# The indexer's logits as three fp32r products of rounded halves instead of one fp32 product

## The reference, cut to what matters

```python
h = x * (1 + scale) + shift
z = h @ w_in                     # qa ka va ga qb kb vb gb qi ki wi
logits = einsum('bthd,bsd->bths', qi, ki) * IDX_DIM ** -0.5    # 8 heads of 64
score  = einsum('bths,bth->bts', relu(logits), wi * 8 ** -0.5)
_, idx = top_k(where(admissible, score, -inf), topk)           # 256 keys (144 for the sample)
```

## Time and profile before

| | us |
|---|---|
| median of 3 runs (lowest, highest) | 1999.81 (1998.09, 2002.83) |
| profiled execution: its time / its span | 2001.68 / 2000.0 |
| PE busy, share of the span | 1869.9, 93% |
| VectorE, ScalarE, GpSimd busy | 979.8, 626.0, 680.4 |
| three query tiles with logits beside them | 284.2 to 392.8 |
| logits of pair 3 alone | 392.8 to 420.9 |
| loop of 32 tiles | 420.9 to about 1229 |

### The profile page before, as it was taken

How to read it: one execution, slowest core, us unless ns; L and a number is a source line. 1 busy time by engine, 2 the same in 40 slices (tenths; PEclk the granted TensorE clock), 3 DMA queues, 4 the chain that set the end, 5 groups by cost and what they waited for, 6 DMA issues and landing times.

```text
span 2000.0 us, 36519 instructions
## 1 busy us (share of the span) xinstructions
PE 1869.9 (93%) x13351; PEld 1561.7 (78%) x13351; DVE 979.8 (49%) x2519; ACT 626.0 (31%) x1359; POOL 680.4 (34%) x860
## 2 busy tenths in 40 slices
PE   5799999999999999999999998989999899999992
PEld 2467887679999999999999996656665688888772
DVE  2244513467777788873000004887777133342726
ACT  1122233421111111111111116988887322122120
POOL 1122211012222222222222224866666543444741
PEclk8899999979999999999999999999999999999996
DMA  7874433113222222222222244431220233346463
GB/s 226 261 250 135 124 98 111 32 38 94 85 89 85 85 86 90 85 85 85 85 85 85 85 120 115 106 84 46 58 52 19 88 121 121 122 124 182 117 216 90
DMA packets 209716, 213.27 MB, mean 107 GB/s; under 512 B 23152, under 2 KB 167280, under 8 KB 208768
## 3 DMA queue, kind: packets, MB, share of 16 engines
q1 hardware_dynamic: 178320, 172.38, 30.4%
q10 hardware_dynamic: 29952, 35.08, 5.0%
q0 software_dynamic: 1328, 4.26, 0.7%
HBM read 181.31 MB, written 34.55 MB: 108 GB/s over the span
## 4 chain that ended last, share of the span: by engine, by line
issue 45%; PE 25%; POOL 18%; ACT 5%; DVE 4%; DMA 3%; POOLq 1%; SPq 0%; ACTq 0%; DVEq 0%
POOL w_lo L1088 8%; POOL w_lo L1137 8%; PE psum L1684 4%; PE psum L1641 3%; PE psum L1663 3%; DMA ada_ring<-in_w_ada_dram 2%; PE psum L1511 2%; PE psum L1469 2%; PE psum L1512 2%; PE psum L1513 2%; ACT p_rows L972 2%; PE psum L1550 2%; PE psum L1552 1%; PE psum L1551 1%; ACT over_z_evacuated L994 1%
## 5 line engine op out<-in xcount | busy, mean ns | idle before, releaser
L1550 PE MATMUL psum<-h_hi,w_hi 128*128 128x364 f32 (+1 forms) x1728 | 577.5, 334 | 6.9 <-POOL w_lo L1088 6.2
L1552 PE MATMUL psum<-h_lo,w_hi 128*128 128x364 f32 (+1 forms) x1728 | 567.7, 329 | 0.0
L1551 PE MATMUL psum<-h_hi,w_lo 128*128 128x364 f32 (+1 forms) x1728 | 566.0, 328 | 0.0
L1088 POOL TENSOR_TENSOR w_lo<-w_raw,w_hi 128x512 fp32r<-128x512 f32 x144 | 185.5, 1289 | 701.5 <-ACT w_hi L831 701.4
L1550 PEld LDWEIGHTS psum<-h_hi,w_hi 128*128 128x128 f32 x1728 | 325.9, 189 | 44.7 <-issue 36.8
L1551 PEld LDWEIGHTS psum<-h_hi,w_lo 128*128 128x128 f32 x1728 | 325.8, 189 | 0.0
L1552 PEld LDWEIGHTS psum<-h_lo,w_hi 128*128 128x128 f32 x1728 | 325.6, 188 | 0.0
L1137 POOL TENSOR_TENSOR w_lo<-w_raw,w_hi 128x512 fp32r<-128x512 f32 x128 | 181.5, 1419 | 209.0 <-ACT w_hi L1017 209.0
L831 ACT ACTIVATE w_hi<-w_raw 128x512 fp32r<-128x512 f32 x144 | 90.7, 630 | 478.2 <-PE psum L1552 454.2
L1253 DVE MAX8 top<-scores 128x8 f32<-128x384 f32 (+6 forms) x210 | 185.4, 883 | 80.1 <-DVE scores L1256 79.9
L1733 PE MATMUL psum<-w_hi,mixed_halves 128*128 128x512 f32 x512 | 202.2, 395 | 11.1 <-POOL w_lo L1137 11.1
(11 more groups left out here) (206 smaller groups left out, 2674.2 us busy)
## 6 DMA issues: line engine op xcount, KB each, us to landing
w_raw<-in_w_in_dram SPq DMA_DIRECT2D x144, 256.0 KB, 2.8
w_raw<-in_w_out_dram SPq DMA_DIRECT2D x256, 128.0 KB, 2.9
z_transposed<-z_evacuated ACTq DMA_DIRECT2D x32, 544.0 KB, 2.7
ada_ring<-in_w_ada_dram SPq DMA_DIRECT2D x64, 256.0 KB, 3.9
ada_ring<-in_w_ada_dram SPq DMA_DIRECT2D x32, 512.0 KB, 5.1
stage<-in_w_ada_dram SPq DMA_DIRECT2D x32, 512.0 KB, 4.0
over_z_evacuated<-z_transposed SPq DMA_DIRECT2D x32, 272.0 KB, 4.5
q_transposed<-z_transposed SPq DMA_DIRECT2D x16, 272.0 KB, 4.8
```

What stands on the lines that cost most here:

```text
L1088: pool.tensor_tensor(v(wlo), raw3[ch][:, :, 0:width], v(whi).bitcast(F32), ALU.subtract).then_inc(lo_ready.sem, 1)
L1550: pe.matmul(Z, w(whi), hh[:, kt_, a:b], start=(kt_ == 0), stop=False)
L1551: pe.matmul(Z, w(wlo), hh[:, kt_, a:b], start=False, stop=False)
L1552: ins = pe.matmul(Z, w(whi), hl[:, kt_, a:b], start=False, stop=(kt_ == KT - 1))
```

## The change

The query halves: ScalarE writes `q_hi` (rounded, two buffers) in place of `z_evacuated`, and VectorE subtracts it from the PSUM bank, three instructions per pair, into `q_lo` (one buffer). The key halves `key_hi` and `key_lo` (1600 columns) are made once on VectorE. The logits of one piece are now six fp32r matmuls, the two heads taking turns: high by high, low query by high key, high query by low key, into the two banks 6 and 7.

```diff
+        def split_q(pair):
+            dve.wait_ge(z_read.sem, z_read.at(pair + 1))
+            dve.wait_ge(l_read.sem, l_read.at(LB + 24 * pair))
+            for c, (a, b) in enumerate(TCH):
+                ins = dve.tensor_tensor(q_lo[:, a:b], bank(3 * (pair % 2) + c)[:, 0:b - a], q_hi[:, pair % 2, a:b].bitcast(F32), ALU.subtract)
+            ins.then_inc(q_split.sem, 1)
+        split_q(0)
+        dve.tensor_copy(key_hi, kidup).then_inc(dve_chain.sem, 1)
+        dve.wait_ge(dve_chain.sem, chained())
+        dve.tensor_tensor(key_lo, kidup, key_hi.bitcast(F32), ALU.subtract).then_inc(key_split.sem, 1)
         n = 0
         for pair in range(4):
+            if pair:
+                split_q(pair)
...
-        n = (len(u) + WCH - 1) // WCH
-        return u[n * ch:n * ch + n]
+        first = 0 if m == NF else 2 if m == NF + 1 else 1
+        n = (len(u) + WCH - first - 1) // (WCH - first)
+        return u[n * (ch - first):n * (ch - first) + n] if ch >= first else []
...
+        def logits(u, n):
+            _, pair, _, t, a, b = u
+            pe.wait_ge(l_read.sem, l_read.at(n))
+            pe.wait_ge(key_split.sem, key_split.at(1))
+            pe.wait_ge(q_split.sem, q_split.at(pair + 1))
+            r, ko = tile_rows(t), 0 if t < NTILE - 1 else PROMPT
+            for i in range(3):
+                for h in range(2):
+                    d = slice(64 * h, 64 * h + 64)
+                    q = q_lo[d, P * t:P * t + r] if i == 1 else q_hi[d, pair % 2, P * t:P * t + r]
+                    k = (key_lo if i == 2 else key_hi)[d, ko + a:ko + b]
+                    ins = pe.matmul(small_bank(n + h)[0:r, 0:b - a], q, k, start=(i == 0), stop=(i == 2))
+                    if i == 2:
+                        ins.then_inc(l_done.sem, 1)
...
-                ins = pe.matmul(B[0:r, 0:b - a], q, kidup[64 * h:64 * h + 64, ko + a:ko + b], start=True, stop=True)
...
                 if b == 0:
                     sp.wait_ge(kv_stored.sem, kv_stored.at(16 * KV_STORES))
+                    sp.wait_ge(l_read.sem, l_read.at(SMALL_UNITS))
```

More of the change, by code:

```diff
@@ L363, in build @@
     line = early[0:16, 672:672 + 2 * NREL].rearrange("p (g n) -> p g n", g=2)
+    s2r = ExitStack()
+    idx_r = sb("indexer_halves", [P, 3648], F32R, where=s2r)
+    stage_r = sb("stage_halves", [P, 2048], F32R, where=s2r)
+    q_hi = sb("z_evacuated_high", [P, 2, TOK], F32R, where=s2r)
+    scores_r = sb("scores_halves", [P, SC_COLS + TOK], F32R, where=s2r)
+    s2r.close()
     s2 = ExitStack()
@@ L368, in build @@
     zev = sb("z_evacuated", [P, 2, TOK], where=s2)
-    scores = sb("scores", [P, SC_COLS + 1024], where=s2)
+    scores = sb("scores", [P, SC_COLS + TOK], where=s2)
     wi_col = sb("wi_columns", [P, NTILE, IDX_HEADS], where=s2)
@@ L373, in build @@
     kidup = idx[:, 0:1600]
+    key_lo = idx_r[:, 0:1600]
+    key_hi = stage_r[:, 0:1600]
+    q_lo = scores_r[:, SC_COLS:SC_COLS + TOK]
     wi_rows = idx[:, 1600:1600 + TOK]
@@ L453, in build @@
     ki_spread = count("ki_spread")
+    key_split = count("key_split", 0)
+    q_split = count("q_split")
     c_silu = count("c_silu")
@@ L932, in _ @@
                 act.wait_ge(l_done.sem, l_done.at(LB + 24 * (m - NF - 1)))
-            z_chunks(m, parity, zev[:, parity, :])
+            z_chunks(m, parity, q_hi[:, parity, :])
         for u in small_after(NH, 0):
@@ L1537, in _, with products @@
                     ada_step(p + 2, u - MOD_UNIT)
-        def products(m, parity, ch, width=P, between=()):
+        def products(m, parity, ch, width=P, between=None):
             pe.wait_ge(lo_ready.sem, lo_ready.at(m * WCH + (ch + 1 - NF * WCH)))
@@ L1544, in products @@
                 pe.wait_ge(z_read.sem, z_read.at(m - NF + (1 - 2)))
+                if between is not None and m > NF + 1:
+                    pe.wait_ge(q_split.sem, q_split.at(m - NF - 1))
             for k in range(WCH):
@@ L1556, in products @@
                     ins.then_inc(w_used.sem, 1)
-                for u in between[2 * k:2 * k + 2 if k < WCH - 1 else None]:
+                for u in (between or [])[2 * k:2 * k + 2 if k < WCH - 1 else None]:
                     small_unit(u)
         ln = [0]
+        def logits(u, n):
[12 more added lines that the diff above has]
+                        ins.then_inc(l_done.sem, 1)
         def small_unit(u):
@@ L1565, in small_unit @@
             B = small_bank(n)
+            if u[0] == "logit":
+                if u[2] == 0:
+                    logits(u, n)
+                return
             pe.wait_ge(l_read.sem, l_read.at(n + 1 - 2))
@@ L1606, in _ @@
         pe.wait_ge(l_read.sem, l_read.at(sum(len(v) for v in SMALL.values())))
+        pe.wait_ge(q_split.sem, q_split.at(4))
         with pe.Fori(0, 8) as r:
```

## The result

The changed kernel is slower: ratio 1.0046 of the time before, 95% interval 1.0036 to 1.0056, so about 9.2 us (7.2 to 11.2) on 1997.7. A second series gave 1.0045 (1.0031 to 1.0060). The medians of the first series are 2009.24 and 1997.71 us, 14 runs each; they lie 11.5 us apart, and the 9.2 us are those of the ratio, which goes by all runs. The profiled execution has a span of 2007.7 us, 7.7 more than before.

A forecast was written before the change was run, and what follows sets the result against it. It took PE's own work to bound three query tiles and a PE-ScalarE chain pair 3. Terms -5.1 + 3.8 + 2.9 + 1.9 + 0.7 - 0.6 = +3.6 us gave 2003.4 us against the median of 1999.8; range 1994 to 2010.

The forecast's parts named there:

- the case "slower": Whole kernel: the changed kernel measures slower than before; chance 0.42.
- the likeliest case: Whole kernel: the summed forecast holds, 2003.4 us with 3 us to either side; chance 0.58.
- Three passes for four: Query tiles of pairs 0 to 2: one pass fewer saves 1.7 us per tile, -5.1 us in all.
- The fixed 0.35 per piece: Each logits piece in the query tiles: gaps before and behind, put down to changing rows, kept whole in fp32r.
- the first rival: Piece borders: with one type throughout the fixed cost goes, -9.0 us, 1994.4 us; chance 0.25.
- Pieces in a row: Tile NF+1, ends of chunks 2 and 3: pieces wait uncovered for both relus of the one before; +3.8 us.
- The handover: Last query tile to pair 3: piece, relus, emptying and subtractions follow one another, 4.36 us instead of 0.98; +2.9 us.
- Pair 3's round trip: Pair 3: 512-wide period 2.20 us at full clock, 2.93 at low, with the second relu waited for; +1.9 us.
- The clock: Pair 3 and loop start: one piece fewer at full clock, +0.7 us; half a possible gain at its return, -0.6.
- The rival of a drop around tile NF+1: Clock drops in tile NF+1, or earlier in pair 3: 2007 us; chance 0.08.
- The heads side by side: Inside each piece: both heads already ran together before, so this brings nothing new; rival without overlap in fp32r 2032 us, chance 0.05.
- weight loads would be bare: Later steps of 48 pieces: two uncovered loads of 0.19 us each, 18 us more, 2022 us; chance 0.04.

The follow-up runs named there:

- the run woven otherwise: Changed kernel with pair 0's pieces spread over chunks 1 to 3 of tile NF+1, none directly behind another; ratio 1.0020, median 2003.91 us.
- The run on it alone: Changed kernel with pair 2's pieces one block of products earlier and queries split range by range behind ScalarE; last product to pair 3's first piece 1.58 us.
- PE kept busy: Changed kernel with useless products added on PE in pair 3, 18 ahead of its first piece and 6 ahead of others; ratio 1.0010.
- head-by-head run: Changed kernel with head 0's three matmuls, then head 1's three, each head waiting for its own bank; ratio 1.0012, pair 3 26.74 us.
- wait-per-bank run: Changed kernel, heads still alternating, but each head waits only for its own bank; pair 3 27.67 us.
- the second trace: The changed kernel run once more, unedited; ratio 1.0045, span 2003.5 us.
- the second trace of before: The kernel before, run again unedited for its trace; pair 3 took 21.45 us, its clock falling only at 416.1.
- the stops mended: Changed kernel with other weaving, earlier pair 2 pieces, range-by-range query split, four banks for pair 3, head-by-head order; ratio 0.9952, median 1989.77 us.

## Why the prediction was right or wrong

The time was inside the range, 2009.24 against 1994 to 2010, and the case "slower" came. Both are partly luck: 0.42 stood against 0.40 for the same, and the range was that wide for the rivals' sake. The number 2003.4 stood for +3.6 us, +9.2 was measured, and the likeliest case's own range (2000.4 to 2006.4) was missed. Step by step:

1. *Three passes for four*: right in kind, -4.3 instead of -5.1. The mis-sized term is the surcharge of a step. I took 0.015 once per piece, but a piece has two steps more and each costs 0.02 over its columns: the seven 512-wide pieces of a tile save 0.16 each (1.05 to 0.89, means of two tiles) where the sum has 0.20, which makes 0.26 of the 0.3 missing. The short pieces matter less: the 128-wide one takes 0.48 us instead of 0.42, the 64-wide one 0.29 instead of 0.26, a loss of 0.09 where the sum comes to 0.05. The fixed 0.35 per piece stayed in fp32r, so the first rival (it goes away, 1994.4) fell on the rows of the 512-wide piece after: the change of rows causes it, not that of type.
2. *Pieces in a row*: right, +3.6 and +3.5 for +3.8; the run woven otherwise wins them back. The 6 us of cover for the halves of the keys, for which they were put in a row, was not needed: its cast was priced at 2.4 us and took 0.98.
3. *The handover*: right, 3.72 us where I had 4.36, +2.4 for +2.9. VectorE's three subtractions take 1.42 for 1.6; ScalarE's emptying starts 0.94 behind the last product for 1.16 and takes 1.18 for 1.40. The run on it alone brings it to 1.58.
4. *Pair 3's round trip*: the step held (2.20 at the full clock, shown with PE kept busy; 2.88 at the low one against 2.93). The head-by-head run and the wait-per-bank run show that the wait for both relus costs 3 to 4 us.
5. *The clock*: this is the step that failed. I had one piece of pair 3 fewer at the full clock (+0.7); there was none to speak of (low from 398.2 in the first trace, from 395.3 in the second), and pair 3 with its clock came to +3.2 and +3.5 where terms 4 and 5 have +2.6. I took half a gain at its return, and the second trace has none. A low stretch costs 0.45 of its length, not half. The rival of a drop around tile NF+1, to which I gave 0.08, came in both traces of the changed kernel and in seven of the eight with that weaving, 1.5 us each, behind the waits of 1.24 and 1.22 us for the relus; that these waits are its cause is supported by the six traces without them, none of which has it, and not more. With the two further pieces at the low clock that belong to it, this rival's 2007 is the nearest of my numbers. And I took one profile of before for the rule, where pair 3's clock was a matter of chance; against the second trace of before the changed kernel's pair 3 is 9.3 us longer, not 3.2.

The heads side by side: right that this was there before; the run head by head shows that it does not even hang on the order. The rule of the Trainium skill (TensorE: Matmul & The Clock Gate, The mechanism) by which weight loads would be bare is not borne out for wide pieces: a step of 512 columns costs 0.235 us with its two loads. The same section of the Trainium skill says that matmuls are "pc-monotone in start AND end — strict FIFO, no reordering". Head by head, head 1's first step stands behind head 0's third in the program and starts with head 0's first (x2 at 342.21); the measurement decides, for matmuls on different rows of the array. The costs I put at nothing (the splits of pairs 0 to 2, SyncE's wait, the later top-k) stayed hidden: up to pair 3 PE waits for nothing but the relus, four times, 4.3 us, and from the loop to the end the changed kernel takes 1579.1 and 1576.6 us against 1578.2 to 1579.0.

## What to carry to other kernels

Where a faster operation sits in a round trip between engines, its passes count for little and the banks between the engines for much. Here four banks instead of two gave 5 us to the kernel that had the slow form and 13 to the one with the fast form, and only with the stops mended do the halves pay (0.9952 against 0.9976; the intervals overlap, the medians of the same set are 1989.77 and 1995.14). And an edit that empties PE for a microsecond or three should be priced with the clock that it may lose, for longer than the gap lasts; one trace does not tell on which side of that edge a stage stands.

## What the runs showed of the hardware that was not expected

- Matmuls on rows 0 to 63 and on rows 64 to 127 run at once even if three of one kind stand ahead of three of the other in the program: 0.90 us per piece in either order.
- Useless products can pay: 84 of them in pair 3 held the clock at 1.00 and made the whole about 7 us shorter.
- A change from 128 rows to 64 and back costs PE about 0.2 us around a piece (starts 0.26 and 0.27 apart instead of 0.166), in fp32r as in fp32.
- The same instructions ran pair 3 at the full clock in one execution (21.45 us) and fell to the low one in two others (27.5 us).
